# Product-key choice of experts: 112 sums a head, two heads alternated, keys found by four heads, expert rows spread anew

## The chip, the core and the metric

One core of one Trainium2 chip. The time is that of one call on the device, in microseconds (us); the metric is the median of the runs.

## What is computed

One decoder block on 512 tokens of 2048 channels, in float32. Attention with a window of 128 and a short convolution are gated and mixed, then a layer norm follows, then the PEER feed-forward part, which the change is about, and a second layer norm. Cut to that part:

```python
h = layer_norm(ALPHA * h + mixed, ln1_g, ln1_b)
q = (h @ w_q).reshape(t, 8, 2, 128)                       # 8 heads, two halves
s = einsum('thpc,hpnc->thpn', q, sub_keys)                # 128 scores a half
top_s, top_i = top_k(s, 16)
cand_s = top_s[:, :, 0, :, None] + top_s[:, :, 1, None, :]            # 16 x 16 sums
cand_i = top_i[:, :, 0, :, None] * 128 + top_i[:, :, 1, None, :]
best_s, best_pos = top_k(cand_s.reshape(t, 8, 256), 16)
expert = take_along_axis(cand_i, best_pos); gate = softmax(best_s)
act = gelu(einsum('cd,chkd->chk', h, u_tab[expert])); y = einsum('chk,chkd->cd', gate * act, v_tab[expert])
out = layer_norm(ALPHA * h + y, ln2_g, ln2_b)
```

## The kernel before

**Stages.** The tokens go in two halves (b = 0, 1) of 256, two tiles of 128 each. Each half passes 82 units of weights of 2 MB (U_K, U_V, eight query units from U_Q, gates and convolution, eight output units from U_OUT = 66, eight PEER query units from U_PQ = 74). Units are numbered n through both halves. From N_U = 164 on the 64 units of the U table follow for half 1 (its experts are computed densely, all 16384), and from N_V = 228 on the 64 units of the V table. TensorE works through them without a break if it can.

**Split weights.** Except for the plain units (half 1 up to U_PQ), a float32 product takes three passes on rounded parts. A unit comes in four quarters j. SP's queue loads it into wbuf[n % 2]; ScalarE (ACT) writes the high part w_hi (split_hi, one buffer, so quarter by quarter behind TensorE); VectorE (split_lo) or GpSimd (low) subtracts it to get w_lo. by_pool says which: the PEER query units of both halves, and N_U and N_U + 1, are GpSimd's. TensorE's split waits for the count of the one or the other.

**Choice of experts.** For each PEER query unit TensorE makes one head's scores in the middle of the next unit (query_scores), ACT copies them to ks (L801; two buffers, so it waits for VectorE's pick_step), and VectorE's pick takes, for two tiles and both halves of the key, the best 16 of 128 (MAX8, FIND_INDEX8 and MATCH_REPLACE8, eight at a time), then adds 256 sums (L1495), takes the best 16 of them (L1501 to L1515), and keeps positions and indices as floats (L1517 to L1526). Each step waits for the one before it. After the eighth head come twelve lookups of 2048 elements (L1553, L1558, L1562), which turn positions into keys; in half 1 eleven split_lo pieces of N_U + 2 to N_U + 4 stand between them.

**Expert rows.** Half 0 isn't computed densely: GpSimd gathers for each of its 256 slots a row tile of U (1 MB) and later of V, 512 in all, and VectorE's take multiplies each (L1180, L1185). rows_in(n) says how many rows VectorE takes in unit n. These rows run beside half 1's work. Three row buffers have memory of their own; up to EARLY_ROWS four more lie over w_hi and act_lo, which are free in the plain units, and after LATE_ROWS two over xT. A gather waits until the row last in its buffer is used. GpSimd's program is one queue: low for the query units of half 0, gathers, low(UNITS + U_PQ), gathers, low for the other units, gathers. Half 1's attention on VectorE follows the rows of its first two units; ACT's exponentials and TensorE's transposes (L1013) wait for it.

**Ahead of the query units.** In output unit c VectorE adds to the residual (L1428), takes rows, and splits ahead. After the eighth it does the layer norm (L1444 to L1458) on which TensorE's transposes (L874) wait.

## Time and profile before

| | |
|---|---|
| median of 3 runs | 3943.13 us (3942.9 to 3957.16) |
| the profiled execution | 3951.56 us |
| its span | 3949.8 us |
| busy: PE, DVE, ACT, POOL | 95%, 70%, 35%, 29% |
| mean granted TensorE clock | 0.982 |

The profile is of one execution. PE is TensorE, PEld its weight loads, DVE VectorE, POOL GpSimd. Its names are those of memory, so the scratch of pick appears as mT. Idle time of an engine is put down to what ended it. Since TensorE is busy nearly throughout, the waits of TensorE and the stretches around them are what is to be read; the halves change at 1055 us, half 1's query units start at 2197, the U table at 2306, the V table at 3178.

### The profile page before, as it was taken

The numbers are of one execution on the slowest core, as the hardware profiler recorded it, in microseconds if no ns is written. First come the engines' busy times: TensorE is split into PE (matmuls) and PEld (weight loads), VectorE is DVE, ScalarE is ACT, GpSimd is POOL, SyncE is SP. The second block draws the span as 40 slices with busy tenths as digits, with TensorE's granted clock in tenths as the row PEclk, the third lists the DMA queues.
The fourth block names the chain that finished last, engine by engine and source line by source line (L and its number), as shares of the span: only waits on it lengthen the run. The fifth ranks groups of instructions, "written<-read, shape, count | busy, mean of one in ns | idle before, by whom it ended". The sixth has DMA issues, their size and how long they took to land.

```text
span 3949.8 us, 61018 instructions
## 1 busy us (share of the span) xinstructions
PE 3766.4 (95%) x24471; PEld 3482.2 (88%) x24471; DVE 2778.0 (70%) x3399; ACT 1379.4 (35%) x1966; POOL 1128.5 (29%) x595
## 2 busy tenths in 40 slices
PE   8999999998979999999999789999998888999997
PEld 8999999998968888888888789999998877778876
DVE  4544555455877765566655897888887888889888
ACT  5544444443323100000000343566663333434432
POOL 0000000003443444444432741211123433345341
PEclk9999999999989999999999999999999999999998
DMA  5245555454598999999999458999999999999996
GB/s 188 106 160 183 185 183 181 181 181 171 184 363 331 388 421 395 407 392 404 397 396 387 178 194 318 356 367 374 363 365 395 395 401 385 408 397 402 411 385 245
DMA packets 209851, 1236.88 MB, mean 313 GB/s; under 512 B 20176, under 2 KB 53536, under 8 KB 66336
## 3 DMA queue, kind: packets, MB, share of 16 engines
q1 hardware_dynamic: 124448, 659.65, 43.8%
q0 software_dynamic: 73728, 536.90, 33.6%
q10 hardware_dynamic: 11520, 38.28, 2.4%
q8 instruction: 95, 1.56, 0.2%
q14 instruction: 60, 0.49, 0.0%
HBM read 1196.48 MB, written 37.75 MB: 312 GB/s over the span
## 4 chain that ended last, share of the span: by engine, by line
PE 78%; DMA 10%; DVE 8%; issue 1%; ACT 1%; POOL 1%; SPq 0%; DVEq 0%; ACTq 0%
PE dense_ps L905 22%; PE dense_ps L894 13%; PE dense_ps L896 12%; PE dense_ps L895 12%; PE dense_ps L1147 6%; DMA wbuf<-in_peer_v_dram 4%; PE score_ps L1147 3%; DMA wbuf<-in_w_units_dram 3%; DMA row<-in_peer_v_dram,expert 3%; DVE h L1185 2%; PE dense_ps L935 2%; PE o_ps L1147 2%; PE oT_ps L1147 2%; PE o_ps L1028 1%; PE score_ps L1104 1%
## 5 line engine op out<-in xcount | busy, mean ns | idle before, releaser
L1231 DVE TENSOR_TENSOR w_lo<-wbuf,w_hi_r 128x1024 fp32r<-128x1024 f32 x800 | 972.0, 1222 | 554.4 <-ACT w_hi_r L549 553.8
L549 ACT ACTIVATE w_hi_r<-wbuf 128x1024 fp32r<-128x1024 f32 x872 | 915.8, 1059 | 1172.2 <-PE dense_ps L896 608.5
L894 PE MATMUL dense_ps<-act_hi,w_hi_r 128*128 128x256 f32 x4128 | 1184.6, 287 | 56.0 <-DVE w_lo L1231 48.8
L895 PE MATMUL dense_ps<-act_lo,w_hi_r 128*128 128x256 f32 x4128 | 1173.6, 284 | 0.0
L896 PE MATMUL dense_ps<-act_hi,w_lo 128*128 128x256 f32 x4128 | 1173.6, 284 | 0.0
L894 PEld LDWEIGHTS dense_ps<-act_hi,w_hi_r 128*128 128x128 f32 x4128 | 797.0, 193 | 68.2 <-DVE w_lo L1231 41.1
L501 POOL DMA_INDIRECT row<-in_peer_v_dram,expert x256 | 499.2, 1950 | 1089.1 <-DVE h L1185 1068.0
L895 PEld LDWEIGHTS dense_ps<-act_lo,w_hi_r 128*128 128x128 f32 x4128 | 797.1, 193 | 0.0
L896 PEld LDWEIGHTS dense_ps<-act_hi,w_lo 128*128 128x128 f32 x4128 | 796.6, 193 | 0.0
L905 PE MATMUL dense_ps<-xT,wbuf 128*128 128x256 f32 x3136 | 686.9, 380 | 0.8 <-ACT xT L534 0.8
L905 PEld LDWEIGHTS dense_ps<-xT,wbuf 128*128 128x128 f32 x3136 | 593.5, 190 | 86.1 <-issue 5.6
L501 POOL DMA_INDIRECT row<-in_peer_u_dram,expert x256 | 445.9, 1742 | 670.6 <-DVE row L1180 572.4
L1185 DVE SCALAR_TENSOR_TENSOR h<-row,dots,h 128x2048 f32<-128x2048 f32 x256 | 604.6, 2362 | 34.0 <-DMA row<-in_peer_v_dram,expert 33.6
L1180 DVE SCALAR_TENSOR_TENSOR row<-row,h 128x2048 f32<-128x2048 f32 x256 | 578.9, 2309 | 32.1 <-DMA row<-in_peer_u_dram,expert 32.1
L492 POOL TENSOR_TENSOR w_lo<-wbuf,w_hi_r 128x1024 fp32r<-128x1024 f32 x72 | 180.5, 2519 | 1005.6 <-ACT w_hi_r L549 1005.5
L1147 PE MATMUL dense_ps<-w_hi_r,e_hi 128*128 128x512 f32 x512 | 162.8, 399 | 32.5 <-DVE w_lo L1231 31.6
L1147 PE MATMUL dense_ps<-w_hi_r,e_lo 128*128 128x512 f32 x512 | 160.4, 395 | 0.0
L1147 PE MATMUL dense_ps<-w_lo,e_hi 128*128 128x512 f32 x512 | 160.0, 394 | 0.0
L761 ACT ACTIVATE stage<-dense_ps 128x512 f32<-128x512 f32 x48 | 28.7, 597 | 361.7 <-PE dense_ps L905 317.2
L1147 PEld LDWEIGHTS dense_ps<-w_hi_r,e_hi 128*128 128x128 f32 x512 | 95.9, 191 | 59.5 <-DVE w_lo L1231 39.8
L894 PE MATMUL dense_ps<-br_hi,w_hi_r 128*128 128x256 f32 x512 | 145.0, 283 | 1.0 <-ACT br_hi L713 1.0
L896 PE MATMUL dense_ps<-br_hi,w_lo 128*128 128x256 f32 x512 | 144.9, 283 | 0.0
(209 smaller groups left out, 4256.0 us busy)
## 6 DMA issues: line engine op xcount, KB each, us to landing
wbuf<-in_w_units_dram SPq DMA_DIRECT2D x456, 1024.0 KB, 6.0
wbuf<-in_peer_v_dram SPq DMA_DIRECT2D x128, 1024.0 KB, 10.2
act_spill<-stage ACTq DMA_DIRECT2D x64, 256.0 KB, 8.5
gate_spill<-gbuf ACTq DMA_DIRECT2D x8, 2048.0 KB, 11.6
e_act<-act_spill SPq DMA_DIRECT2D x32, 512.0 KB, 11.3
e_gate<-gate_spill SPq DMA_DIRECT2D x32, 512.0 KB, 12.7
cT<-in_x_dram SPq DMA_DIRECT2D x2, 2048.0 KB, 10.1
row<-in_peer_u_dram,expert POOLq DMA_INDIRECT x256, 13.9
```

The costliest lines, as they stand in the source:

```text
L492: nc.gpsimd.tensor_tensor(w_lo[n % 2][:, j, :], wbuf[n % 2][:, j, :], w_hi[:, j, :].bitcast(F32), ALU.subtract).then_inc(lo_by_pool, 1)
L501: pool.indirect_dma_start(out=row[SLOT[g]][:, :], out_offset=None, in_=(u_tab if g < U_ROWS else v_tab)[:, :], in_offset=bass.IndirectOffs ...
L549: act.activation(w_hi[:, j, :], wbuf[n % 2][:, j, :], ACT.Copy).then_inc(w_hi_ready, 1)
L894: nc.tensor.matmul(out, w[0], x[0], start=opens, stop=False)
L895: nc.tensor.matmul(out, w[0], x[1], start=False, stop=False)
L896: return nc.tensor.matmul(out, w[1], x[0], start=False, stop=closes)
L905: last = nc.tensor.matmul(dense_ps[n % 4][:, c, :], w_part(wbuf[n % 2], n, k, j), src[:, k, :], start=opens and k == 0, stop=closes and k ...
L935: last = nc.tensor.matmul(dense_ps[n % 4][:, t, :], src[:, k, tok], w_part(wbuf[n % 2], n, k, j), start=t == 0 and k == 0, stop=t == TILES ...
L1147: last = nc.tensor.matmul(ffn_ps[t][j % 2 * 2 + c], e[:, blk, tok], w[:, j, c * 512:(c + 1) * 512], start=opens and j < 2 and at == 0, sto ...
L1180: V.scalar_tensor_tensor(out=row[slot][:, :], in0=row[slot][:, :], scalar=1.0, in1=h0[:, t, :], op0=ALU.mult, op1=ALU.mult, accum_out=dots ...
L1185: V.scalar_tensor_tensor(out=h0[:, t, :], in0=row[slot][:, :], scalar=dots[:, t, col:col + 1], in1=h0[:, t, :], op0=ALU.mult, op1=ALU.add) ...
L1231: V.tensor_tensor(w_lo[n % 2][:, j, :], wbuf[n % 2][:, j, :], w_hi[:, j, :].bitcast(F32), ALU.subtract).then_inc(lo_by_dve, 1)
```

## The change

- A head adds 112 sums in place of 256: the first four of one side with all 16 of the other, and the other twelve with the first four. No other pair can be among the best 16.
- pick(c) alternates the key steps of head c with the sum steps of head c - 1; ks has eight buffers, over aT, and ACT's wait for pick_step is gone.
- Keys are found four heads at a time by find_keys(0), behind pick(4), and find_keys(1), behind the last. Each works on both tiles, with six operations of 2048 elements and seven small ones ahead, which turn a position among 112 into two places. expert becomes ready by four heads for both tiles.
- Of the eleven w_lo pieces between the lookups three are left, N_U + 2's first three, in the last third of find_keys(1); section takes the others.
- The unit U_PQ of both halves is split by VectorE, its fourth piece behind the layer norm.
- Rows: 4 and 5 in the first two units of half 1 (0 and 12 before), 6 in each attention unit (5), 3 in U_PQ - 2 (5), none in U_PQ (3), one each in five of the query units, behind pick, and one each in N_U + 2 and N_U + 3. The last stage keeps 108 (115).
- GpSimd gathers the first three rows ahead of its wait for dense_ready, keeps three gathers ahead in half 1's query units, and issues them between the low calls.

```diff
 def by_pool(n, j):
 
-    return U_PQ <= n < UNITS or UNITS + U_PQ <= n < N_U + 2
+    return U_PQ < n < UNITS or UNITS + U_PQ < n < N_U + 2
...
     if j >= 0:
-        return 0 if j < 4 else 2 if j < G_FIRST + 32 else 3
-    if r < U_V or r > U_PQ or r == U_PQ - 1:
-        return 0
-    if r >= U_PQ - 2:
-        return 5 if r < U_PQ else 3
+        return 0 if j < 2 else 1 if j < 4 else 2 if j < G_FIRST + 32 else 3
     if r < U_Q:
-        return 12
+        return 4 + r
     if r < U_GA:
-        return 5
-    return 4 if r % 4 == 0 else 3
+        return 6
+    if r < U_PQ - 2:
+        return 4 if r % 4 == 0 else 3
+    return {U_PQ - 2: 3, U_PQ + 1: 1, U_PQ + 2: 1, U_PQ + 3: 1, U_PQ + 5: 1, U_PQ + 6: 1}.get(r, 0)
...
-        ks = scratch(0, 1024).rearrange("p (n t a k) -> p n t a k", n=2, t=2, a=2)
-        ksw = scratch(1024, 512).rearrange("p (t a k) -> p t a k", t=2, a=2)
...
+        ks = aT[:, :, :].rearrange("p k t -> p (k t)").rearrange("p (c t a k) -> p c t a k", c=PH, t=TILES, a=2)
+        onehot = scratch(0, 2048).rearrange("p (s k) -> p s k", k=TOPK)
...
             def gather(g):
 
                 t, col = g // SLOTS % TILES, g % SLOTS
-                if g < U_ROWS and col == 0:
-                    pool.wait_ge(expert_ready, t + 1)
+                if g in (0, SLOTS // 2):
+                    pool.wait_ge(expert_ready, 2 * g // SLOTS + 1)
...
-            for n in range(U_PQ, UNITS):
+            for n in range(U_PQ + 1, UNITS):
                 low(n)
+            for g in range(3):
+                gather(g)
             pool.wait_ge(dense_ready, UNITS)
-            for g in range(ROWS_TO[UNITS + U_PQ - 1]):
-                gather(g)
-            low(UNITS + U_PQ)
-            for g in range(ROWS_TO[UNITS + U_PQ - 1], ROWS_TO[UNITS + U_PQ]):
+            for g in range(3, ROWS_TO[UNITS + U_PQ - 2] + 3):
                 gather(g)
             for n in range(UNITS + U_PQ + 1, N_U + 2):
                 low(n)
-            for g in range(ROWS_TO[UNITS + U_PQ], LATE_ROWS):
+                for g in range(ROWS_TO[n - 3] + 3, ROWS_TO[n - 2] + 3):
+                    gather(g)
+            for g in range(ROWS_TO[N_U - 1] + 3, LATE_ROWS):
                 gather(g)
...
-                    act.wait_ge(pick_step, 12 * (at_ - 2) + 2 + START)
-                    act.activation(ks[:, c % 2, :, :, :].rearrange("p t a k -> p (t a k)"),
+                    act.activation(ks[:, c, :, :, :].rearrange("p t a k -> p (t a k)"),
                                    score_ps[c % 2][:, :, :].rearrange("p t k -> p (t k)"), ACT.Copy).then_inc(ks_out, 1)
                     split_hi(n + 2, 2)
...
-                    split_lo(n + 1, 3)
+                    if c < 7:
+                        split_lo(n + 1, 3)
                     split_lo(n + 2, 0)
...
-                rows(n0 + U_PQ)
-
...
+                split_lo(n0 + U_PQ, 3)
+
+                def pick(c):
+
+                    first, second = c < PH, c > 0
+                    f, g = 4 * (PH * b + c), 5 * (PH * b + c - 1)
+                    both = [(t, a) for t in range(TILES) for a in range(2)]
+                    d = c - 1
+                    if first:
+                        at_k = lambda t, a, k: topi[:, c // 4, a, t, c % 4, k:k + 8]
+                        dve.wait_ge(ks_out, PH * b + c + 1 + START)
+                        dve.wait_ge(sums_step, 5 * (PH * b + c - 2) + 1 + START)
                         for t, a in both:
-                            last = V.max(tops[:, t, a, 0:8], sc[:, t, a, :])
+                            last = V.max(tops[c % 2][:, t, a, 0:8], ks[:, c, t, a, :])
                         last.then_inc(pick_step, 1)
-                        step(1)
+                    if second:
+                        top = tops[d % 2]
+                        at_p = lambda t, k: bestp[:, d // 4, t, d % 4, k:k + 8]
+                        dve.wait_ge(pick_step, f + START)
+                        if b or d >= 4:
+                            dve.wait_ge(key_step, 11 * (2 * b + d // 4))
+
+                        V.tensor_tensor(cand[:, :, 0:64].rearrange("p t (a b) -> p t a b", b=TOPK),
+                                        top[:, :, 0, 0:4].unsqueeze(3).to_broadcast([P, TILES, 4, TOPK]),
+                                        top[:, :, 1, :].unsqueeze(2).to_broadcast([P, TILES, 4, TOPK]), ALU.add)
+                        V.tensor_tensor(cand[:, :, 64:112].rearrange("p t (a b) -> p t a b", b=4),
+                                        top[:, :, 0, 4:TOPK].unsqueeze(3).to_broadcast([P, TILES, TOPK - 4, 4]),
+                                        top[:, :, 1, 0:4].unsqueeze(2).to_broadcast([P, TILES, TOPK - 4, 4]), ALU.add
+                                        ).then_inc(sums_step, 1)
+                    if first:
+                        dve.wait_ge(pick_step, f + 1 + START)
                         for t, a in both:
-                            V.max_index(topi[:, t, a, 0:8], tops[:, t, a, 0:8], sc[:, t, a, :])
+                            V.max_index(at_k(t, a, 0), tops[c % 2][:, t, a, 0:8], ks[:, c, t, a, :])
                         for t, a in both:
-                            last = V.match_replace(ksw[:, t, a, :], tops[:, t, a, 0:8], sc[:, t, a, :], LOWEST)
+                            last = V.match_replace(ksw[:, t, a, :], tops[c % 2][:, t, a, 0:8], ks[:, c, t, a, :], LOWEST)
                         last.then_inc(pick_step, 1)
-                        step(2)
+                    if second:
+                        dve.wait_ge(sums_step, g + 1 + START)
+                        for t in range(TILES):
+                            last = V.max(best[:, t, d, 0:8], cand[:, t, :])
+                        last.then_inc(sums_step, 1)
...
+                    if second:
+                        dve.wait_ge(sums_step, g + 2 + START)
+                        for t in range(TILES):
+                            V.max_index(at_p(t, 0), best[:, t, d, 0:8], cand[:, t, :])
+                        for t in range(TILES):
+                            last = V.match_replace(candw[:, t, :], best[:, t, d, 0:8], cand[:, t, :], LOWEST)
+                        last.then_inc(sums_step, 1)
...
+                        dve.wait_ge(sums_step, g + 3 + START)
...
+                            last = V.max(best[:, t, d, 8:16], candw[:, t, :])
+                        last.then_inc(sums_step, 1)
+                        dve.wait_ge(sums_step, g + 4 + START)
...
-                            last = V.max_index(bestp[:, t, 8:16], bests[:, t, 8:16], candw[:, t, :])
...
+                            last = V.max_index(at_p(t, 8), best[:, t, d, 8:16], candw[:, t, :])
+                        last.then_inc(sums_step, 1)
+
+                def find_keys(w):
+
...
+                    at_ = bestp[:, w, :, :, :].rearrange("p t h k -> p (t h k)")
+                    V.tensor_scalar(pos_4, at_, 4, None, ALU.logical_shift_right)
+                    V.tensor_scalar(pos_2, at_, 2, None, ALU.logical_shift_right).then_inc(key_step, 1)
+                    V.tensor_copy(topf, topi[:, w, :, :, :, :].rearrange("p a t h k -> p a (t h k)"))
...
+                    V.scalar_tensor_tensor(out=place_of[0], in0=pos_2, scalar=-12.0, in1=pos_4, op0=ALU.add, op1=ALU.max
...
+                    V.tensor_scalar(row_at, place_of[0], 4.0, 48.0, ALU.mult, ALU.add).then_inc(key_step, 1)
...
+                    V.scalar_tensor_tensor(out=row_0, in0=place_of[0], scalar=16.0, in1=row_at, op0=ALU.mult, op1=ALU.min
...
+                    V.tensor_tensor(place_of[1], at_, row_0, ALU.subtract).then_inc(key_step, 1)
+                    dve.wait_ge(key_step, f + 5)
+                    for a in range(2):
+                        V.tensor_tensor(onehot, place_of[a].unsqueeze(2).to_broadcast([P, 128, TOPK]),
+                                        iota[:, 0:TOPK].unsqueeze(1).to_broadcast([P, 128, TOPK]), ALU.is_equal
+                                        ).then_inc(key_step, 1)
+                        if b and w and a:
+                            split_lo(N_U + 2, 0)
+                        dve.wait_ge(key_step, f + 6 + 3 * a)
...
+                        V.tensor_tensor(oh, oh, num.unsqueeze(2).to_broadcast([P, 8, TOPK, TOPK]), ALU.mult
...
+                        if b and w and a:
+                            split_lo(N_U + 2, 1)
...
+                        V.tensor_reduce(key_of[:, a, :, 64 * w:64 * w + 64], onehot.rearrange("p (t s) k -> p t s k", t=TILES),
...
+                        if b and w and a:
+                            split_lo(N_U + 2, 2)
...
+                    if not b:
+                        V.scalar_tensor_tensor(out=expert[:, :, 64 * w:64 * w + 64], in0=key_of[:, 0, :, 64 * w:64 * w + 64],
...
+                for c in range(PH + 1):
+                    pick(c)
+                    if c == 4:
+                        find_keys(0)
+                    if b and c < PH:
+                        rows(n0 + U_PQ + c)
...
-                def split_during(k):
-
-                    n, j = N_U + 2 + (k - 1) // 4, (k - 1) % 4
-                    if b and k < 12:
-                        split_lo(n, j)
...
+                find_keys(1)
...
-                if n > N_U + 2 and n + 1 < N_V + U_UNITS:
+                if n > N_U and n + 1 < N_V + U_UNITS:
                     split_lo(n + 1, 3)
                 for j in range(3):
-                    if n > N_U + 2 and n + 2 < N_V + U_UNITS:
+                    if n > N_U and n + 2 < N_V + U_UNITS:
                         split_lo(n + 2, j)
```

## Rows read from the trace of the kernel before

**Rows 1.** Waits of TensorE, whole span: us in total, times, longest.
```profile
PE dense_ps L894 <- DVE w_lo L1231: 48.8, 27, 9.3
...
PE dense_ps L1147 <- DVE w_lo L1231: 31.6, 14, 10.2
...
PE score_ps L874 <- DVE cT L1458: 18.9, 1, 18.9
```

**Rows 2.** Timelines of ScalarE, GpSimd, TensorE, first change: start, us, instruction, idle before.
```profile
1025.03 0.58 ACT L801 ACTIVATE mT<-score_ps 128x512 f32<-128x512 f32 x1
...
1044.75 2.41 POOL L492 TENSOR_TENSOR w_lo<-wbuf,w_hi_r 128x1024 fp32r<-128x1024 f32 x1 [0.97 <-ACT w_hi_r L549]
...
1090.11 2.25 POOL L501 DMA_INDIRECT row<-in_peer_u_dram,expert  x1 [42.95 <-issue]
...
1140.61 2.17 PE L1013 MATMUL dense_ps<-ident,mT 128*128 128x128 f32 x8 [22.84 <-ACT mT L682]
```

**Rows 3.** Timeline of VectorE in the same stretch.
```profile
1062.80 0.87 DVE L1478 MAX8 mT<-mT 128x8 f32<-128x128 f32 x4 [0.26 <-DVE mT L1526]
...
1068.22 0.74 DVE L1495 TENSOR_TENSOR mT<-mT 128x256 f32<-128x256 f32 x2
...
1074.62 0.43 DVE L1534 TENSOR_TENSOR gate<-mT 128x256 f32<-128x256 f32 x1
...
1104.48 2.29 DVE L1180 SCALAR_TENSOR_TENSOR row<-row,h 128x2048 f32<-128x2048 f32 x1
...
1138.26 0.42 DVE L1275 CUSTOM_DVE_ANT_0 mT<-score_ps,mask 128x256 f32<-128x256 f32 x1
```

**Rows 4.** Windows: length, busy PE, PEld, DVE, ACT, POOL, clock, DMA share, GB/s.
```profile
1118.00:1140.00 22.00, 0.00 (x0) 0.00 (x0) 17.69 (x24) 0.05 (x1) 12.84 (x8) 0.59 1.01 422
...
1143.00:1145.00 2.00, 2.00 (x9) 1.19 (x9) 0.18 (x1) 0.57 (x2) 0.00 (x0) 0.50 1.05 438
...
1200.00:1250.00 50.00, 50.00 (x303) 43.63 (x299) 35.98 (x84) 18.08 (x61) 13.85 (x11) 1.00 0.88 337
...
3180.00:3924.00 744.00, 712.14 (x3065) 581.70 (x3063) 645.19 (x450) 291.20 (x286) 296.61 (x117) 0.98 0.98 388
...
3340.00:3360.00 20.00, 20.00 (x90) 16.57 (x89) 16.60 (x11) 7.22 (x7) 6.71 (x4) 1.00 1.03 412
```

**Rows 5.** Groups by line and form, whole span: busy us, mean ns; idle before.
```profile
L1553 DVE TENSOR_TENSOR mT<-mT,iota 128x2048 f32<-128x2048 f32 x8 | 18.3, 2290 | 0.1
...
L1478 DVE MAX8 mT<-mT 128x8 f32<-128x128 f32 x64 | 14.0, 281 | 21.0 <-ACT mT L801 19.9 <-DVE mT L1526 1.0
...
L1501 DVE MAX8 mT<-mT 128x8 f32<-128x256 f32 x32 | 12.1, 419 | 2.7 <-DVE mT L1495 0.5
```

**Rows 6.** Timeline of VectorE in half 1, beside GpSimd.
```profile
2165.35 0.69 DVE L1428 SCALAR_TENSOR_TENSOR cT<-cT,stage 128x512 f32<-128x512 f32 x1 [5.30 <-ACT stage L777]
...
2174.31 7.95 DVE L1180 SCALAR_TENSOR_TENSOR row<-row,h 128x2048 f32<-128x2048 f32 x1 [2.40 <-DMA row<-in_peer_u_dram,expert]
...
2189.38 0.68 DVE L1428 SCALAR_TENSOR_TENSOR cT<-cT,stage 128x512 f32<-128x512 f32 x1
...
2231.14 3.98 DVE L1495 TENSOR_TENSOR mT<-mT 128x256 f32<-128x256 f32 x2
```

**Rows 7.** Timelines of ScalarE, VectorE and TensorE up to the second change of stage.
```profile
2178.53 0.60 ACT L777 ACTIVATE stage<-dense_ps 128x512 f32<-128x512 f32 x1 [2.40 <-PE dense_ps L935]
...
2275.86 0.87 DVE L1478 MAX8 mT<-mT 128x8 f32<-128x128 f32 x4 [0.26 <-ACT mT L801]
...
2293.37 0.60 ACT L792 ACTIVATE stage<-dense_ps 128x512 f32<-128x512 f32 x1 [1.82 <-PE dense_ps L896]
...
2305.78 0.60 ACT L792 ACTIVATE stage<-dense_ps 128x512 f32<-128x512 f32 x1 [1.82 <-PE dense_ps L896]
...
2338.97 0.55 PE L894 MATMUL dense_ps<-act_hi,w_hi_r 128*128 128x256 f32 x1 [9.29 <-DVE w_lo L1231]
...
2379.46 0.58 PE L894 MATMUL dense_ps<-act_hi,w_hi_r 128*128 128x256 f32 x1 [3.71 <-DVE w_lo L1231]
```

More of the change, by code:

```diff
@@ L192, in build @@
         gate = sb("gate", [P, HALVES, TILES, SLOTS])
-        cols = sb("cols", [P, 2, 16], U32)
+        tops = [sb(f"tops{i}", [P, TILES, 2, TOPK]) for i in range(2)]
         dots = sb("dots", [P, TILES, SLOTS])
@@ L339, in build @@
         pick_step = sem("pick_step")
+        sums_step = sem("sums_step")
+        key_step = sem("key_step")
         gather_step = sem("gather_step")
@@ L1460, in _ @@
                     split_transposes(2 * b + 1, 4 * c, 4 * c + 4)
-                rows(n0 + U_PQ)
-                def pick(i, part=0):
-                    for c in range(4):
-                        n = UNITS * b + U_PQ + 4 * part + c
-                        f = 12 * (8 * b + 4 * part + c)
-                        sc = ks[:, c % 2, :, :, :]
-                        both = [(t, a) for t in range(TILES) for a in range(2)]
-                        def step(k):
-                            dve.wait_ge(pick_step, 48 * i + (f + k + START))
-                            dve.sem_inc(went_on, 1)
-                        dve.wait_ge(ks_out, 4 * i + (8 * b + 4 * part + c + 1 + START))
-                        dve.sem_inc(went_on, 1)
+                split_lo(n0 + U_PQ, 3)
@@ L1491, in pick @@
+                    if first:
+                        dve.wait_ge(pick_step, f + 3 + START)
                         for t, a in both:
-                            last = V.max_index(topi[:, t, a, 8:16], tops[:, t, a, 8:16], ksw[:, t, a, :])
+                            last = V.max_index(at_k(t, a, 8), tops[c % 2][:, t, a, 8:16], ksw[:, t, a, :])
                         last.then_inc(pick_step, 1)
+                    if second:
+                        dve.wait_ge(sums_step, g + 3 + START)
@@ L1512, in pick @@
-                        last.then_inc(pick_step, 1)
-                        step(8)
-                        for t in range(TILES):
-                            last = V.max_index(bestp[:, t, 8:16], bests[:, t, 8:16], candw[:, t, :])
-                        last.then_inc(pick_step, 1)
-                        V.tensor_copy(best[:, :, bass.ds(4 * i + (4 * part + c), 1), :].rearrange("p t o k -> p (t o) k"), bests
-                                      ).then_inc(pick_step, 1)
-                        step(9)
```

104 lines of the change are left out of this document (37 added, 67 removed).

## Prediction

> **What bounds the kernel now.** I read the waits of TensorE first, then the timelines of the engines around its long waits, then windows by stage. TensorE is busy for 95% of the span, so only its waits and its half-speed stretches can be won, and each wait has to be read where it stands. The largest [rows 1] are for w_lo pieces of VectorE (48.8 us in 27 waits, 9.3 the longest), the same in the last stage (31.6), and one of 18.9 for the second layer norm. The fourth is the 22.8 us before the first attention step of half 1, from 1117.8 to 1140.6 [rows 2]. In it VectorE never rests: it picks heads until 1074.6, looks up keys and norms the gates until 1104.5, and takes 12 expert rows until 1138.3 [rows 3]. TensorE's granted clock is at its lower level, 1.2 of 2.4 GHz, after the idle stretch (0.50 at 1143) [rows 4]; it stays there for some 5 us, so a long wait costs about 2.5 us more than its length. The last stage is different: for 744 us the DMA engines are at 0.98 of their time, while TensorE does in a full stretch 90 matmuls in 20 us [rows 4], so 64 units of 48 could pass in 683 us. That stage is limited by bytes.
>
> **Price of a head and of a key search.** Head 7 of half 0 stands free of other engines: 1062.8 to 1074.6 is 11.8 us, 5.4 for the keys and 6.4 for the sums [rows 3]. Ten of the sum instructions shrink from 256 to 112 elements. A MAX8 goes from 281 to 419 ns between 128 and 256 elements [rows 5], 1.1 ns an element, so each saves 0.15: 1.5 us. The two additions save 0.3. The copy, the two shifts and the two casts behind them (1.1 us) leave the head. Alternating two heads fills most of the 0.15 us gaps between dependent steps: 1.1. That leaves 7.8 us a head, and 3.3 for the last half step, in which nothing alternates. The lookup keeps twelve operations of 2.29 us [rows 5], now six in each find_keys, but each call adds seven small ones, some 2.4 us with their gaps: 16.4 us a call, 33 a half where there were 28.
>
> **The lock.** Beside POOL's w_lo subtractions some VectorE instructions wait. The two additions that take 0.75 together [rows 3] took 3.98 in half 1, and a row multiplication of 2.3 [rows 3] took 7.95 while POOL worked [rows 6]. MAX8 in the same stretch keeps its length. So each exposed addition, copy, shift or row waits for a POOL piece of 2.4 us [rows 2] when POOL is due. The Trainium skill, SBUF — State Buffer, "Who interferes with whom", says that GpSimd and VectorE exclude each other for whole instructions where VectorE has two SBUF inputs or a two-port mode, and that tensor_reduce never takes part; the additions and the rows agree with it, and the reduction isn't seen beside POOL here. Find_keys(0) now runs in the middle of the query units, where POOL splits.
>
> **A: first change of stage.** Head 4's scores are copied at 1025.6 [rows 2]. Pick(4) 7.8, lock 1.1: 1034.5. Find_keys(0) 16.4 and 0.3 for expert; POOL has four pieces left until 1047.2 [rows 2], 9.0 of lock: 1060.2. Pick(5) to pick(7) 23.4, last half 3.3, gate 0.4: 1087.3. Find_keys(1) 16.7, gate sums 1.2: 1105.2. So the rows start no earlier than now. But the gathers no longer start at 1090.1 [rows 2]: the first four heads' experts exist at 1060, seven rows land long before, and it is 9 rows at 2.21, not 12 with DMA waits: 1125.1. From the mask to TensorE it is 2.35 [rows 2, 3]: 1127.5 in place of 1140.6, **13 us won**. Bounds: no lock, 10 us earlier, which TensorE reaches only to 1117.8, 25 with the clock; 7 if the heads cost a tenth more.
>
> **B: second layer norm.** ACT has copied the last output unit at 2179.1, VectorE takes it at 2189.4 [rows 6, 7], held by five rows, whose gathers waited for a slot not yet free, and by the lock with POOL's split of U_PQ. Changed: addition of c = 6 at 2165.35 as before [rows 6], splits of U_PQ by VectorE as ACT delivers, row 258 to 2172.9, splits to 2177.3, rows 259 and 260 to 2182.0. The wait of 18.9 falls by **7.4** (5 to 8). In half 0 those three splits lie in 9 us of VectorE idle: nothing. The fourth split, behind the norm, takes 1.2 us, and is needed 3 us later.
>
> **C: second change of stage.** Times are the trace's, less B. Head 4's scores come at 2268.4 (2275.8 now) [rows 7]. Pick(4) with 1.6 of lock: 2277.8. Find_keys(0) 16.4, lock 10 (small ones 4, three of the four large two-input ones 2 each): 2304.2. Pick(5) and its row: 2314.4. On POOL, the gather behind low(U_PQ + 7) reuses the slot of that row (264), and low(N_U) is queued behind the gather. So POOL waits for VectorE: gather 2, piece 2.4, and TensorE, free since 2305.7 - 7.4 = 2298.4 [rows 7], starts N_U at 2318.9: **a new wait of 20.5**. It runs N_U in 12.4 (from copy to copy) [rows 7] + 2.5 (clock) and N_U + 1, without scores, in 11.5: 2345.3. VectorE: pick(6), row, pick(7) (its scores come only in the middle of N_U, 2328.8), last half and gate: 2341.8. In find_keys(1) the first split of N_U + 2 stands behind 2.4 + 7.0 + 2.3, and takes 1.2: 2354.7, against 2339.0 now [rows 7]: 15.7 later, B included. But before, the twelve lookups with eleven splits among them still follow, and TensorE loses 3.7 before 2379.5 [rows 7], 0.8 in three short waits ahead of it, and 2.6 of clock. These 7.1 go. **B and C together lose 8.6.** Bounds: without lock N_U starts at 2307.2 and N_U + 2 at 2341.5: 4.6 won. With every small instruction behind a whole POOL piece: 20 lost.
>
> **D: rows.** By my count of rows_in, 57 rows are done by the end of the queries (52 before), 266 (261) at N_U, 404 (397) at the last stage, which keeps 108 in place of 115. Seven rows of 1.05 MB at 412 GB/s [rows 4] are 18 us of a stage without spare DMA time; I take **17** (bounds 0 and 20). The Trainium skill, SBUF — State Buffer, "Summary: rules for kernel authors", would have transfers from HBM reckoned at about 358 GB/s; that would make the seven 20.5. The windows show 412 in a full stretch. The queries of half 1 take eight rows more: VectorE is at 72% there and DMA at 0.88 [rows 4], 18 us of rows in 177 us fit; I put 1 us (0 to 6) for it.
>
> **Waits and queues.** ACT's wait for pick_step ahead of its score copy goes with the eight buffers; it ended no wait of TensorE, so nothing. VectorE's new waits for sums_step and key_step are for work that is ahead of them on VectorE itself; only the chain inside find_keys has gaps, which are counted. The one queue where a new wait holds others is POOL's, in C.
>
> **The sum.** -13 + 8.6 - 17 + 1 = -20.4. The profiled execution took 3951.6 (span 3949.8), 8.4 over the median of 3943.1. From its time 3931, from the median **3923**.
>
> **The rivals.**
> No lock on the new operations: is_equal and mult read broadcast inputs, which the trace doesn't show beside POOL. A gives 25, B and C win 4.6: -47 with D, 3896. Against: the additions read broadcasts too [rows 6]. Chance 0.20.
> Rows free nothing: the stage could be held by slots and VectorE (645 of 744 us busy [rows 4]) rather than bytes. Then -3, 3940. Against: DMA 0.98. Chance 0.20.
> The POOL queue holds longer: each small instruction of find_keys(0) meets a piece, and the gathers behind the low pieces of U_PQ + 3 to 5 stall TensorE too. B and C lose 20: -9, 3934. Chance 0.07.
> Slower: the head. Both changes of stage run at VectorE's pace, four heads each behind the scores of head 4, so each us a head costs 8. If alternating and narrowing bring nothing, and a head costs its 11.8 as now, it is +32: +12, 3955. The point of change is 10.3 us a head. For it: two additions alone took 3.98 beside POOL [rows 6]. Against: its instructions are narrower or gone. Chance 0.06.
> Forecast 0.47. Something under 0.5% (19.7 us) is about what a measurement of this kernel can't tell from no change. The forecast's own range, 3910 to 3936, lies on both sides of 3923.4; 0.27 of it is faster. With the first rival: faster 0.47, same 0.49, slower 0.04. The range: from the first rival's centre, 3896, to 3945, which takes in the second and third.
>
> **What would show it.** The wait at L1013 falls to about 10; that of the second norm to 11; a wait for POOL w_lo of about 20 at the start of N_U and one for VectorE w_lo of about 9 at N_U + 2; the last stage shorter by 17 with DMA still near 1. A stall at N_U under 10 would refute the lock; an unchanged last stage would refute D. Additions of 2 to 4 us in half 1, and is_equal of 4 or more beside POOL, would be the lock itself.

## The result: the change doesn't pay, and the profile after

Before 3946.2 us, after 3956.1 us (medians of 20 runs each on the same chips); the ratio is 1.0023 with a 95% interval of 1.0012 to 1.0034, some 9 us slower, where the forecast was 20 us faster. The profiled execution has a span of 3956.6 against 3949.8, so 6.8 us have to be found. Line numbers of after lie two or three above those of before. The waits of TensorE over the whole span, as in [rows 1]: engine and line, who was waited for, us in total, times, longest.

```profile
PE dense_ps L896 <- DVE w_lo L1233: 49.2, 24, 14.8
PE dense_ps L896 <- POOL w_lo L494: 35.3, 4, 20.6
PE dense_ps L1149 <- DVE w_lo L1233: 24.5, 17, 3.6
PE score_ps L876 <- DVE cT L1461: 11.5, 1, 11.5
...
PE dense_ps L1015 <- ACT mT L685: 4.3, 1, 4.3
```

Three waits fell: the one ahead of attention from 22.8 to 4.3, that of the second norm from 18.9 to 11.5, those of the last stage from 31.6 to 24.5. One is new: 35.3 us for GpSimd's pieces.

A wait tells what was lost, not when the loss was made good. So I followed one event through both traces: ScalarE's copy of a unit's result (stage<-dense_ps, the same copy in both). The table has the difference, after minus before, at such copies; A to D are the terms of the forecast:

| place | before | after | difference | gained or lost since |
|---|---|---|---|---|
| first attention step of half 1 and on to 2062 | 1333.5 | 1315.9 | -17.6 | A: -17.6 |
| behind a wait for weights at 2065 | 2137.1 | 2123.4 | -13.7 | +3.9 |
| first query units, behind the second norm | 2218.0 | 2197.2 | -20.8 | B: -7.1 |
| N_U + 4 | 2385.0 | 2411.5 | +26.6 | C: +47.4 |
| N_U + 60 | 3131.5 | 3154.3 | +22.8 | -3.8 |
| end of the span | 3949.8 | 3956.6 | +6.8 | D: -16.0 |

So A, B and D came out near the forecast, and one stretch, C (167 us long before, 214 after), lost 47 us where 16 were expected. Half 0 first, VectorE's timeline and TensorE's (start, us, instruction, idle before it), as in [rows 2, 3]:

```profile
1056.90 0.86 DVE L1477 MAX8 tops<-aT 128x8 f32<-128x128 f32 x4
...
1064.26 0.85 DVE L1477 MAX8 tops<-aT 128x8 f32<-128x128 f32 x4
...
1079.67 0.27 DVE L1486 TENSOR_TENSOR mT<-tops 128x128 f32<-128x128 f32 x1
...
1100.25 2.29 DVE L1182 SCALAR_TENSOR_TENSOR row<-row,h 128x2048 f32<-128x2048 f32 x1
...
1120.17 0.42 DVE L1277 CUSTOM_DVE_ANT_0 mT<-score_ps,mask 128x256 f32<-128x256 f32 x1
```

```profile
1122.51 2.17 PE L1015 MATMUL dense_ps<-ident,mT 128*128 128x128 f32 x8 [4.29 <-ACT mT L685]
```

Heads 5, 6 and 7 take 22.8 us together (1056.90 to 1079.67), 7.6 each where head 7 took 11.8 [rows 3]; the rows start at 1100.25 and end at 1120.17. Now half 1, GpSimd and VectorE from the second to the seventh head:

```profile
2228.49 0.95 POOL L503 DMA_INDIRECT row<-in_peer_v_dram,expert  x1 [2.42 <-DVE h L1187]
2229.46 9.49 POOL L494 TENSOR_TENSOR w_lo<-wbuf,w_hi_r 128x1024 fp32r<-128x1024 f32 x4
2248.01 0.95 POOL L503 DMA_INDIRECT row<-in_peer_v_dram,expert  x1 [9.06 <-DVE h L1187]
2248.99 9.39 POOL L494 TENSOR_TENSOR w_lo<-wbuf,w_hi_r 128x1024 fp32r<-128x1024 f32 x4
2267.44 0.95 POOL L503 DMA_INDIRECT row<-in_peer_v_dram,expert  x1 [9.07 <-DVE h L1187]
2268.41 14.13 POOL L494 TENSOR_TENSOR w_lo<-wbuf,w_hi_r 128x1024 fp32r<-128x1024 f32 x6
```

```profile
2217.75 1.32 DVE L1486 TENSOR_TENSOR mT<-tops 128x128 f32<-128x128 f32 x1
...
2225.38 2.84 DVE L1187 SCALAR_TENSOR_TENSOR h<-row,dots,h 128x2048 f32<-128x2048 f32 x1
...
2230.16 8.95 DVE L1486 TENSOR_TENSOR mT<-tops 128x128 f32<-128x128 f32 x1
...
2245.41 2.33 DVE L1187 SCALAR_TENSOR_TENSOR h<-row,dots,h 128x2048 f32<-128x2048 f32 x1
...
2248.45 10.08 DVE L1486 TENSOR_TENSOR mT<-tops 128x128 f32<-128x128 f32 x1
...
2267.87 12.41 DVE L1486 TENSOR_TENSOR mT<-tops 128x128 f32<-128x128 f32 x1
```

Read the two side by side. The gather at 2228.49 has waited for the row of 2225.38 (its releaser is DVE h L1187). Only then does GpSimd start its four pieces (a piece is the subtraction for one quarter of a unit; several without a gap are called a run here), and they take 9.49 us. The next head's first addition, 0.27 us when free (1079.67), starts inside that run and ends with it: 8.95 us. (The next two start while the gather is being issued, 0.4 us behind its start, and are kept out by the run behind it all the same.) So the head, and the row behind it, are late; the next gather waits 9.06 us for that row; the next run starts late; and so on. It is a circle: **gather, run, addition, row, gather**, with a period of 19.4 us (2248.45 to 2267.87) where TensorE needs 12.4. Five additions (8.95, 10.08, 12.41 and, behind the search, 10.07 and 10.05) take 51.6 us. What TensorE sees of it:

```profile
2251.48 0.44 PE L896 MATMUL dense_ps<-act_hi,w_hi_r 128*128 128x256 f32 x1 [4.67 <-POOL w_lo L494]
...
2318.60 0.55 PE L896 MATMUL dense_ps<-act_hi,w_hi_r 128*128 128x256 f32 x1 [20.61 <-POOL w_lo L494]
...
2338.00 0.55 PE L896 MATMUL dense_ps<-act_hi,w_hi_r 128*128 128x256 f32 x1 [4.69 <-POOL w_lo L494]
...
2367.11 0.55 PE L896 MATMUL dense_ps<-act_hi,w_hi_r 128*128 128x256 f32 x1 [14.82 <-DVE w_lo L1233]
```

With one of 5.29 at 2270.91 and one of 5.41 at 2383.13 these six waits come to 55.5 us, against 14.2 in the same stretch before (13.0 in the two of [rows 7], the rest in short ones); the other 6.1 of the 47.4 fit TensorE's lower clock behind them, for the mean granted clock from 2197 to 2374 was 0.86, and 0.96 before.

### The profile page after: what moved, and what is told of

Read it like the earlier page. It is cut to its first block, busy times and chain, and to the rows that moved or that the text cites. A ratio compares the mean times of both kernels' runs of the same rounds, so it can differ in the third digit from the quotient of the medians.

```text
span 3956.6 us, 60806 instructions
## 1 busy us (share of the span) xinstructions
PE 3770.0 (95%) x24471; PEld 3483.3 (88%) x24471; DVE 2783.5 (70%) x3355; ACT 1382.1 (35%) x1966; POOL 1099.4 (28%) x587
## 4 chain that ended last, share of the span: by engine, by line
PE 78%; DVE 10%; DMA 9%; issue 1%; ACT 1%; SPq 0%; ACTq 0%; DVEq 0%
PE dense_ps L907 22%; PE dense_ps L896 12%; PE dense_ps L898 12%; PE dense_ps L897 12%; PE dense_ps L1149 6%; DMA wbuf<-in_peer_v_dram 3%; DMA row<-in_peer_v_dram,expert 3%; PE score_ps L1149 3%; DVE h L1187 2%; PE dense_ps L937 2%; DMA wbuf<-in_w_units_dram 2%; PE o_ps L1149 2%; PE oT_ps L1149 2%; PE o_ps L1030 1%; DVE mT L1486 1%; PE score_ps L1106 1%
## 5 line engine op out<-in xcount | busy, mean ns | idle before, releaser
L1233 DVE TENSOR_TENSOR w_lo<-wbuf,w_hi_r 128x1024 fp32r<-128x1024 f32 x808 | 982.2, 1222 | 573.6 <-ACT w_hi_r L552 572.1
L1187 DVE SCALAR_TENSOR_TENSOR h<-row,dots,h 128x2048 f32<-128x2048 f32 x256 | 601.2, 2348 | 27.8 <-DMA row<-in_peer_v_dram,expert 27.2
L494 POOL TENSOR_TENSOR w_lo<-wbuf,w_hi_r 128x1024 fp32r<-128x1024 f32 x64 | 157.8, 2487 | 1002.5 <-ACT w_hi_r L552 1002.4
L1149 PE MATMUL dense_ps<-w_hi_r,e_hi 128*128 128x512 f32 x512 | 162.5, 399 | 25.2 <-DVE w_lo L1233 24.5
L897 PE MATMUL dense_ps<-br_lo,w_hi_r 128*128 128x256 f32 x512 | 144.9, 283 | 0.0
## 6 DMA issues: line engine op xcount, KB each, us to landing
gate_spill<-gbuf ACTq DMA_DIRECT2D x8, 2048.0 KB, 11.5
```

What stands on the lines that cost most here:

```text
L494: nc.gpsimd.tensor_tensor(w_lo[n % 2][:, j, :], wbuf[n % 2][:, j, :], w_hi[:, j, :].bitcast(F32), ALU.subtract).then_inc(lo_by_pool, 1)
L897: nc.tensor.matmul(out, w[0], x[1], start=False, stop=False)
L1149: last = nc.tensor.matmul(ffn_ps[t][j % 2 * 2 + c], e[:, blk, tok], w[:, j, c * 512:(c + 1) * 512], start=opens and j < 2 and at == 0, sto ...
L1187: V.scalar_tensor_tensor(out=h0[:, t, :], in0=row[slot][:, :], scalar=dots[:, t, col:col + 1], in1=h0[:, t, :], op0=ALU.mult, op1=ALU.add) ...
L1233: V.tensor_tensor(w_lo[n % 2][:, j, :], wbuf[n % 2][:, j, :], w_hi[:, j, :].bitcast(F32), ALU.subtract).then_inc(lo_by_dve, 1)
```

## The experiments

Theory LOOP: the circle above costs C's extra. Rivals: the search in the middle of the units (SEARCH), the rows between the heads (ROWS), the form of the addition (FORM). e1, e3, e4, e7, e9 and e12 differ from the changed kernel only by the edit shown or described, e2, e5 and e8 from e1, e6 from e5, e10 from e6, e11 from e10. Ratios are to the kernel before, measured beside each on the same chips, with their 95% interval; the changed kernel has 1.0023 (1.0012 to 1.0034). The groups ran on different chips, so kernels of different groups are compared by their ratios.

| kernel | median us | ratio to before |
|---|---|---|
| e1_gathers_later | 3929.6 | 0.9947 (0.9933 to 0.9962) |
| e2_waits_stay | 3934.3 | 0.9968 (0.9945 to 0.9991) |
| e3_search_at_end | 3946.8 | 0.9997 (0.9982 to 1.0012) |
| e4_additions_by_tile | 3957.0 | 1.0009 (0.9988 to 1.0029) |
| e7_spacer | 3950.5 | 1.0017 (1.0002 to 1.0031) |
| e9_wait_behind_gather | 3941.3 | 0.9993 (0.9976 to 1.0010) |
| e12_plain_copy | 3948.8 | 1.0011 (0.9997 to 1.0024) |
| e8_rows_late | 3928.7 | 0.9981 (0.9957 to 1.0006) |
| e5_splits_ahead | 3912.7 | 0.9922 (0.9899 to 0.9945) |
| e6_searches_last | 3898.6 | 0.9893 (0.9877 to 0.9910) |
| e10_fed | 3900.9 | 0.9875 (0.9854 to 0.9897) |
| e11_rows_in_gate_units | 3896.4 | 0.9877 (0.9859 to 0.9894) |

**e1_gathers_later: break the circle.** The first pair of lines is the loop's, the second that of the loop behind it.

```diff
-                for g in range(ROWS_TO[n - 3] + 3, ROWS_TO[n - 2] + 3):
+                for g in range(max(ROWS_TO[n - 5], ROWS_TO[UNITS + U_PQ - 2]) + 3, max(ROWS_TO[n - 4], ROWS_TO[UNITS + U_PQ - 2]) + 3):
-            for g in range(ROWS_TO[N_U - 1] + 3, LATE_ROWS):
+            for g in range(ROWS_TO[N_U - 3] + 3, LATE_ROWS):
```

> The changed kernel, with the gathers of half 1's query units issued two units later (behind low of c + 5 in place of c + 3); rows, picks and searches stay. Theory LOOP: in the changed kernel the gather makes GpSimd wait for a row that VectorE takes behind pick(c), GpSimd is then late and splits four pieces in one run, the next head's first addition (normally 0.27 us) waits 9 to 12 us for the whole run, and so the next row is late again. With the gathers later that wait is gone: the first additions of half 1 fall to 1 to 3 us, the waits of TensorE for GpSimd's w_lo (35 us) vanish, N_U starts some 30 us earlier, and one of 16 to 26 us for VectorE's w_lo at N_U + 2 takes part of it back. Time 3915 to 3930. Rival SEARCH: the cost is find_keys(0), 16 us in the middle of the query units, which this kernel leaves there; then heads 5 to 7 stay late and the time stays above 3945. Rival ROWS: the rows taken between the heads cost it; then unchanged as well, 3950 to 3960.

As LOOP says: 3929.6, at the upper end of its range, with rows and search where they were, so SEARCH and ROWS fall. There is no wait for GpSimd in C, N_U's result comes 36.7 us earlier (2296.7 for 2333.4), and a wait of 34.2 for VectorE's first split of N_U + 2 takes part of that back, more than the 16 to 26 expected: N_U + 4 is 23.7 earlier. Pieces and VectorE's instructions now take turns, here in VectorE's timeline of e1:

```profile
2230.72 2.46 DVE L1489 TENSOR_TENSOR mT<-tops 128x96 f32<-128x96 f32 x1
...
2278.51 4.37 DVE L1562 TENSOR_TENSOR mT<-mT,uconv 128x2048 f32<-128x2048 f32 x1
2282.91 2.29 DVE L1567 TENSOR_REDUCE mT<-mT 128x128 f32<-128x2048 f32 x1
```

The addition (0.25 when free) has waited 2.2 us, for one piece; the mult of 2.29 has waited 2.1, and the reduction, with GpSimd busy, not at all. Find_keys(0) took 26.2 us (2270.17 to 2296.39). That is the lock of the forecast, which gave 26.4. (The profiled execution of e1 was the slowest of its eight, 3942.3.)

**e2_waits_stay: is it the wait or the gather?** As e1, with this where the gather stood:

```diff
+                if ROWS_TO[n - 2] > ROWS_TO[n - 3] and n > UNITS + U_PQ + 2:
+                    pool.wait_ge(row_used, FREE[ROWS_TO[n - 3] + 3] + START)
```

> As e1_gathers_later (gathers two units later), but GpSimd still waits for the row at the place where the gather stood. LOOP as stated (the wait is what counts): as the changed kernel, 3956 within 4, first additions of 9 to 12 us. If the gather instruction itself is the cause (that VectorE can't get in behind it), the additions fall to 1 to 3 us and the time is that of e1_gathers_later.

3934.3, so LOOP in the form that I had written down is wrong: a GpSimd that is late isn't enough. The trace holds both cases, GpSimd's timeline and VectorE's:

```profile
2240.20 9.57 POOL L494 TENSOR_TENSOR w_lo<-wbuf,w_hi_r 128x1024 fp32r<-128x1024 f32 x4 [3.31 <-DVE h L1189]
2253.87 0.95 POOL L503 DMA_INDIRECT row<-in_peer_v_dram,expert  x1 [4.09 <-DVE h L1189]
2254.84 9.48 POOL L494 TENSOR_TENSOR w_lo<-wbuf,w_hi_r 128x1024 fp32r<-128x1024 f32 x4
```

```profile
2240.98 1.77 DVE L1488 TENSOR_TENSOR mT<-tops 128x128 f32<-128x128 f32 x1
...
2254.30 10.18 DVE L1488 TENSOR_TENSOR mT<-tops 128x128 f32<-128x128 f32 x1
```

Both runs are four pieces without a gap behind a wait for the row. Into the first the addition gets after one piece (1.77). Ahead of the second stands a gather, and the addition waits for all of it (10.18). In this kernel it is so in all five additions behind the first row that met a run: 0.7, 1.8 and 1.9 us without a gather ahead, 10.2 and 10.1 with one.

**e3_search_at_end.** `if c == 4` becomes `if c == (8 if b else 4)`, and the additions' wait for key_step follows.

> The changed kernel, with find_keys(0) of half 1 moved from behind pick(4) to behind pick(8); gathers stay. LOOP: the runs of GpSimd and the long additions stay, one head every 19.4 us, and both searches now stand ahead of the splits of N_U + 2: the first of these comes some 12 us later, time 3962 to 3970. SEARCH: the heads then keep step with the scores, no addition over 3 us, and N_U starts without a wait: 3920 to 3930.

The additions are as long as before (8.91, 10.05, 12.37, 10.12, 10.03), which is against SEARCH. But the time, 3946.8, is below what LOOP expected: N_U waited 6.8 us, not 20.6, since GpSimd's wait for the row behind the search is gone, and the first split of N_U + 2 came at 2362.2, not at 2377. Two causes stood in that place, and I had priced the one and forgotten what the other gave back.

**e4_additions_by_tile.** The 128x128 addition as a loop over two of 128x64.

> The changed kernel, with the first addition (128x128, both tiles in one instruction) made as two of 128x64, one a tile, as in the kernel before. LOOP with the run as what holds VectorE: the first of the two waits 9 to 12 us, the second 0.2, time 3956 within 4. Rival FORM: it is the form of the one instruction that doesn't get in between two GpSimd pieces (in the kernel before, two additions took 3.98 us beside GpSimd); then each of the two waits for one piece at most, under 5 us together, GpSimd is late by less, and the time falls by 20 to 35.

9.01, 10.12 and 12.45 us for the two, 3957.0: FORM falls. These waits also show how long VectorE is kept out. The run behind the gather at 2266.58 has five pieces (11.7 us); then GpSimd waits 0.20 us for ScalarE, and there the addition gets in, ahead of the sixth piece.

**e7_spacer, e9_wait_behind_gather, e12_plain_copy: what is it about the gather?** In the loop, behind the gather (e7 and e9) or in place of its indirect DMA (e12, for the five gathers between pieces; the rows copied are not the experts', so that part of the output isn't computed):

```diff
+                    pool.memset(spare[:, g % 8:g % 8 + 1], 0.0)
```

```diff
+                    pool.wait_ge(row_in[SLOT[g]], 16 * USE[g])
```

```diff
+                    pool.dma_start(out=row[SLOT[g]][:, :], in_=v_tab[P * (g % 8):P * (g % 8 + 1), :]).then_inc(row_in[SLOT[g]], 16)
```

> The changed kernel, with one tiny GpSimd instruction (a memset of 128x1) behind each of the gathers that stand between its pieces. In e2_waits_stay the long addition (10.2, 10.05 us) came where a gather stood right ahead of GpSimd's run of pieces, and the addition was 0.7 to 1.9 us, one piece at most, where GpSimd had waited without a gather. Theory NEXT (a run that directly follows a gather isn't interrupted, any other instruction between ends that): additions at most 2.5 us, time 3932 to 3940. Rival STATE (what the gather leaves lasts until GpSimd next has to wait): additions of 9 to 12 us as in the changed kernel, 3956 within 4.

> The changed kernel, but behind each gather between its pieces GpSimd waits until that row has landed, some 2.5 us, before it goes on with its run. Theory STATE, which e7_spacer left standing (a GpSimd run behind a gather isn't interrupted until GpSimd next has to wait): the wait ends it, so the additions of half 1 are at most 2.5 us each although GpSimd starts its runs 2.5 us later still; the heads come every 12.4 us again where find_keys(0) doesn't stand, N_U starts at least 15 us earlier than in the changed kernel, and the time is 3930 to 3942. If the long additions come only of GpSimd being late (its pieces all due at once), they stay at 9 to 12 us, and the time is 3956 or more.

> The changed kernel, with the five gathers between GpSimd's pieces in half 1 replaced by plain copies of 128 rows of the same size, issued on GpSimd's queue at the same places behind the same waits; five experts' rows are thus wrong ones, so that part of the output isn't computed. Theory INDIRECT (what holds VectorE comes of the indirect gather, whose addresses GpSimd works out): behind a plain copy a run is interrupted after one piece, additions at most 2.5 us, time 3930 to 3942, as with the waits alone. Rival ANY (every DMA that GpSimd issues ahead of a run does it): additions of 9 to 12 us, 3956 within 4.

The spacer changes nothing (8.95, 10.10, 12.42): NEXT falls. GpSimd and VectorE in e9, with the wait:

```profile
2224.99 0.95 POOL L503 DMA_INDIRECT row<-in_peer_v_dram,expert  x1 [2.42 <-DVE h L1188]
2232.89 11.41 POOL L494 TENSOR_TENSOR w_lo<-wbuf,w_hi_r 128x1024 fp32r<-128x1024 f32 x4 [6.95 <-DMA row<-in_peer_v_dram,expert]
```

```profile
2233.25 4.12 DVE L1188 SCALAR_TENSOR_TENSOR h<-row,dots,h 128x2048 f32<-128x2048 f32 x1
```

All additions behind the first take 0.27 us there, but most of them fall into GpSimd's waits, which shows little. Two (2263.94 and 2310.81) start while a gather is being issued, as in the changed kernel, and aren't kept out when a wait follows it. The rows say more: three start inside a run behind a gather and its wait, and they get in after one piece (4.12, 3.12 and 3.09 us, 2.33 when free). So STATE holds, on three cases. The time, 3941.3, is at the slow end of what was expected, because GpSimd waited 4.7 to 7.2 us for a row's landing and not 2.5. Part of the expectation missed: TensorE waited 36.8 us for GpSimd all the same, and N_U's result came at 2333.2 as in the changed kernel (2333.4), not 15 us earlier.

The plain copy acts as the gather does (8.61, 9.72, 12.03, 9.70 and 9.70 us), so INDIRECT falls too. Of the times, 3950.5 for e7 and 3948.8 for e12 lie 2 and 3 us below the range of the rival that holds, 3952 to 3960; their ratios can't be told from the changed kernel's. GpSimd and VectorE in e12:

```profile
2224.67 0.59 POOL L502 DMA_DIRECT2D row<-in_peer_v_dram  x1 [2.45 <-DVE h L1191]
2225.28 9.51 POOL L494 TENSOR_TENSOR w_lo<-wbuf,w_hi_r 128x1024 fp32r<-128x1024 f32 x4
```

```profile
2226.33 8.61 DVE L1490 TENSOR_TENSOR mT<-tops 128x128 f32<-128x128 f32 x1
```

So where GpSimd has issued a DMA, of either kind, ahead of a run of its pieces, VectorE was kept out until GpSimd next had to wait. What in the chip does it the runs don't show. One place in e1 goes the other way: at 2277.12 a run behind a gather had to wait for VectorE's lookup, which was already under way, and from then on the two took turns.

**e8_rows_late.** As e1, with `2 if j < G_FIRST + 39 else 3` for `G_FIRST + 32`.

> e1_gathers_later, with seven rows moved back from the gate stage to the last stage (two a unit instead of three for seven more units), so that it holds 115 rows as in the kernel before. Theory BYTES (the last stage is limited by DMA, a row costs 1.05 MB at 412 GB/s there): 17 us more than e1_gathers_later, 3947 (3942 to 3952). Rival FREE (rows in the last stage cost nothing; slots or VectorE hold it): as e1_gathers_later, 3930 within 3.

By the medians nothing changed (3928.7 and 3929.6), by the ratios e8 is 13 us slower, with intervals that overlap; two of its eight runs were 16 and 27 us above its median. Neither 17 us more nor a clean tie is shown. The traces say more. From N_U + 8 to N_U + 60 e8 takes 680.9 us, where eight kernels without this edit (after, e1 to e7) take 693.4 to 702.5, 698 in the mean. From there to the end it takes 809.3, and the kernel before, with 115 rows too, 818.3, where those eight, with 108 rows, take 790.7 to 804.1, 798 in the mean. So the seven rows are worth some 17 us in the one stage and 11 to 20 in the other; by bytes they are 18. In both stages the DMA engines are at 0.98 to 1.00 of their time (the first from 3000 to 3130), and a row only changes its place. BYTES is right about each stage and wrong about the sum.

**e5_splits_ahead and e6_searches_last: can the freed time be had?** In e1 TensorE stands 34.2 us for a split whose high part ScalarE delivered near 2301. The helper below takes eleven splits: five ahead of the last heads, as shown, and six in find_keys(1) in place of three. The section behind takes only what is left.

```diff
+                pieces = [(N_U + 2 + k // 4, k % 4) for k in range(11)] if b else []
+                def ahead(count=1):
+                    for _ in range(count):
+                        if pieces:
+                            split_lo(*pieces.pop(0))
...
+                    if c == 7:
+                        ahead(3)
+                    if c == 8:
+                        ahead(2)
                     pick(c)
```

> e1_gathers_later, with eleven of VectorE's splits (N_U + 2 to N_U + 4) taken ahead among the last heads and the lookups of half 1: three before pick(7), two before pick(8), six in find_keys(1), in place of three in its second half. In e1_gathers_later TensorE stands 34.2 us at N_U + 2 for the first of them, which VectorE takes at 2341, though ScalarE has delivered it near 2301. Theory ORDER (the wait is only VectorE's order of work, it has time to spare): that wait falls to about 4, followed by three or four of 3 us and one split every 3.5 us where TensorE needs one every 2.9; together 18 in place of 40. Time 3908 (3900 to 3916). Rival FULL (VectorE is full until the searches end, and the wait only moves): 8 to 10 won, 3920.

> e5_splits_ahead, but find_keys(0) of half 1 moves from behind pick(4) to just ahead of find_keys(1), and fifteen splits stand among the two searches and before pick(8). In e1_gathers_later find_keys(0) lasted 26.2 us beside GpSimd (2270.2 to 2296.4), 16.4 without it in half 0. Theory LOCK (the 10 us between are VectorE waiting for GpSimd's pieces, one each): behind the last piece of GpSimd the search costs 16.4 again, the heads keep step with the scores, and TensorE waits under 10 us in all at the second change of stage; 3898 (3890 to 3906), 10 less than e5_splits_ahead. If the long waits for VectorE's splits have another cause, it is as e5_splits_ahead.

e5: 3912.7, within its range; of the wait 12.4 remained, not 4, as VectorE reached the splits ahead of pick(7) only at 2322.6. All waits of TensorE for VectorE between 2190 and 2430 fell from 39.6 to 19.0 us. TensorE in e1 and in e5:

```profile
2342.39 0.55 PE L896 MATMUL dense_ps<-act_hi,w_hi_r 128*128 128x256 f32 x1 [34.17 <-DVE w_lo L1233]
```

```profile
2323.95 0.55 PE L896 MATMUL dense_ps<-act_hi,w_hi_r 128*128 128x256 f32 x1 [12.37 <-DVE w_lo L1233]
```

e6 has both searches behind the gate's subtraction and fifteen splits, three ahead of pick(8) and twelve among the searches: 3898.6 as forecast, by the ratio 42 us below the kernel before. Each search costs 15 to 16 us without its splits, and TensorE waits 11.5 us for VectorE in all between 2190 and 2430, where under 10 were expected.

**e10_fed and e11_rows_in_gate_units.** `range(15)` becomes 23 in e10, with one split ahead of each row up to N_U + 5; e11 adds a row in every fourth gate unit (`2 if j < G_FIRST + 32 and (j < G_FIRST or j % 4) else 3`).

> e6_searches_last with 23 splits in place of 15 interleaved, one ahead of each lookup step and of each row up to N_U + 5. In e6_searches_last the fifteen end at 2355, and TensorE waits 8.6 us at N_U + 5 (VectorE norms the gates and takes two rows first), with some 2.5 us of lower clock. Theory ORDER: that wait goes, 3888 (3884 to 3893), about 10 less than e6_searches_last. Rival FULL: VectorE has too much to do until 2420, and the wait comes a few units later: 3896 to 3900.

> e10_fed with eight rows taken from the last stage and put into the 32 units of the gate stage, one more in every fourth unit, where the DMA engines are at 0.91 to 0.93 of their time and not at 1.0. e8_rows_late showed that rows moved between the last stage and the units just before it change nothing, since both are full. Theory BYTES with room (only a row that goes where DMA has time to spare is won): 11 to 18 us less than e10_fed. Rival: VectorE (84% busy there, 2.35 us a row) feeds TensorE late, and what is won behind is lost there: as e10_fed within 4.

Both miss: 3900.9 and 3896.4 can't be told from 3898.6, and by the ratios the two are 6 to 7 us below e6 with intervals that overlap. In e10 the wait of 8.6 went (7.6 us in 15 waits are left, 2.3 the longest). N_U + 8 came 9.9 us earlier than in e6, but N_U had come 5.1 earlier already, so 4.8 are the edit's; at N_U + 60 only 1.2 of the 9.9 were left. In e11 the last stage took 791.7 us, 9 less than in e10, but the kernels with 108 rows differ by 13 us there, and eight rows are 20 us by bytes. Why neither gain shows stays open. That the time behind N_U is now set by bytes would fit e10 but isn't shown, and e11 speaks against its simple form. The best version is any of the three, 1.07 to 1.25% below the kernel before.

## Why the prediction was wrong

**The lock.** This is the step that failed: "each exposed addition, copy, shift or row waits for a POOL piece of 2.4 us". One piece is right where no DMA of GpSimd stands right ahead of the run (e1, e2) or where GpSimd has waited behind it (e9). Behind a DMA it is the run up to GpSimd's next wait: five additions took 51.6 us, where 1.6 each, the forecast's price for pick(4), would have been 8. The number was in the prediction's own rows. It called a row of 7.95 us a wait for one piece; 7.95 less 2.3 is 5.6, more than two pieces. GpSimd in the kernel before:

```profile
2172.18 0.94 POOL L501 DMA_INDIRECT row<-in_peer_v_dram,expert  x1 [2.30 <-DVE row L1180]
2173.15 11.31 POOL L492 TENSOR_TENSOR w_lo<-wbuf,w_hi_r 128x1024 fp32r<-128x1024 f32 x4
```

The gather stands right ahead of the run, and the row got in only behind the third piece, where GpSimd had to wait for ScalarE's fourth high part (ready at 2180.08). A price that is more than its unit should have been asked why.

**C.** Forecast +16 with B left out, measured +47.4. The chain of causes was right (gather behind the row, low behind the gather, TensorE behind low). That its largest link came out at 20.6 us, with 20.5 forecast, was luck, for two errors cancelled: find_keys(0) started at 2288.9, not at 2277.8, as the heads before it were late by the circle, and it lasted 16.2 us, not 26.4, since GpSimd stood still. I took the loop through the queue once, at N_U. It closes on itself in every unit in which a row is taken behind a head, and each turn costs 7 us. Without the circle (e1) N_U + 4 came 23.7 us earlier; the rest of C's loss lay in the order of VectorE's splits, and e6, with both mended, had N_U + 4 at 2348.9 where the changed kernel had it at 2411.5. The third rival (the POOL queue holds longer) had this place and direction (gathers behind the low pieces of U_PQ + 3 to 5) at 0.07 and 3934, with the same one-piece price.

**A.** Forecast -13, measured -17.6, of which 3.9 went again at 2065. The rows started at 1100.25, not 1105.2: the lock took 6.6 of find_keys(0) and not 9.0, and the heads and the second search were together some 2.5 cheaper than priced. The loss of 3.9 wasn't in the forecast. DMA is now full in this window (length, busy time of PE, PEld, DVE, ACT, POOL, clock, DMA share, GB/s), where it was at 0.94 in the same units before, and a wait for weights at 2065 grew from 2.2 to 3.4 us. That the one caused the other is likely and not shown. Behind 2.2 the granted clock stayed at 1.00; behind 3.4 it was 0.50, the lower of its levels, 1.2 of 2.4 GHz, which cost another 2.6.

```profile
1182.00:1382.00 200.00, 199.53 (x1082) 174.94 (x1081) 152.31 (x250) 46.10 (x141) 90.12 (x57) 1.00 1.00 397
...
2065.00:2068.00 3.00, 2.81 (x7) 2.29 (x8) 3.00 (x5) 0.00 (x0) 2.30 (x1) 0.50 1.04 434
```

**B.** Forecast -7.4, measured -7.1; the wait is 11.5, as written.

**D.** Forecast -17, measured -16.0, right for a reason that e8 makes likely. Five of the seven rows went into half 1, where DMA stood at 0.88 in attention [rows 4] and at 0.45 in the query units (2180 to 2300), and two to N_U + 2 and 3. The rival "rows free nothing" is refuted for these rows (798 against 809 and 818 us). The last stages of kernels with the same 108 rows differ by up to 13 us, so the size is softer than the figure looks.

**Price of a head.** 7.8 forecast, 7.6 measured; the last half step 3.2 (3.3), the search 15.9 to 16.2 (16.4). The slower rival (a head that costs 11.8 as now, 3955) came closest in its time and is wrong in its cause.

**The first rival** (no lock on the new operations) is refuted by the mult of 4.37 us and an is_equal of 4.43 in e1, and by a mult of 4.38 at 1042.98 in half 0 of the changed kernel. The Trainium skill, SBUF — State Buffer, "Who interferes with whom", has the exclusion by whole instructions: the turns in e1 agree, and the reduction there took no part. The runs behind a DMA go beyond it, and there the measurement decides.

**Sum.** -17.6 + 3.9 - 7.1 + 47.4 - 3.8 - 16.0 = +6.8, the difference of the two spans.

## What to carry to other kernels

When a queue gets a step that waits for another engine, follow what the delay does to that engine in turn: if the queue's own work holds the engine up, the two drive each other, and the price is paid at every round. A gather that only has to be early enough can be issued two units later for nothing, and a search whose result is not needed yet belongs behind the work that feeds TensorE; together with splits taken in order of need that turned +0.2% into -1.1%. Before moving transfers out of a full stage, look at the DMA share of the stage that they go to.

## What the hardware showed that I had not expected

- Behind a DMA that GpSimd had issued, indirect or plain, its run of pieces kept a VectorE addition out until GpSimd next had to wait: 8.6 to 12.4 us in 27 cases of six kernels, 0.4 to 2.5 us without the DMA.
- An instruction of GpSimd between the DMA and the run doesn't end that (e7), a wait for the DMA's landing does (e9, three rows).
- A wait of 3.4 us put TensorE's granted clock to 0.50 for some 5 us; one of 2.2 us left it at 1.00. The length alone doesn't decide it: in the last stage of the changed kernel one of 3.59 us (up to 3809.90) left it at 1.00, and behind one of 1.84 (up to 3514.39) it was 0.50.
- Seven rows moved between two stages at full DMA gave some 17 us to the one and cost the other 11 to 20, and the medians stayed.
